# Sample softmax of two heads on 128 partitions, with shared transpositions, in a hybrid encoder step

## The reference, cut to what matters

```python
def fox_block(q, k, v, f_q, f_k, q_pos, k_pos):          # branch B
    s = jnp.einsum('bqhd,bkhd->bhqk', q, k).astype(jnp.float32) * (HEAD_DIM ** -0.5)
    s = s + jnp.swapaxes(f_q, 1, 2)[..., :, None] - jnp.swapaxes(f_k, 1, 2)[..., None, :]
    mask = k_pos[None, :] <= q_pos[:, None]
    s = jnp.where(mask[None, None], s, NEG_INF)
    p = jax.nn.softmax(s, axis=-1).astype(v.dtype)
    return jnp.einsum('bhqk,bkhd->bqhd', p, v)

def band_attention(q, k, v, q_pos, k_pos, rel_bias):     # branch A
    s = jnp.einsum('bqhd,bkhd->bhqk', q, k).astype(jnp.float32) * (HEAD_DIM ** -0.5)
    s = s + rel_bias.astype(jnp.float32)[:, rel][None]
    ...
    p = jax.nn.softmax(s, axis=-1).astype(v.dtype)
    return jnp.einsum('bhqk,bkhd->bqhd', p, v)

# sample: q has 64 rows, k and v have 1024 + 64 (B) or 512 + 64 (A) rows; prompt: 512 rows, causal or banded
```

## Time and profile before

| what | value |
|---|---|
| runs | 2879.72, 2883.22, 2882.98 us |
| profiled execution | 2885.47 us, its span 2883.7 us |
| PE | 2807.5 us busy, 97% of the span |
| PE weight loads | 2641.2 us, 92% |
| DVE | 1320.6 us, 46% |
| ACT | 985.1 us, 34% |
| POOL | 108.6 us, 4% |
| DMA | 112 GB/s mean |

### The profile page before, as it was taken

How to read it: one execution, slowest core, us unless ns; L and a number is a source line. 1 busy time by engine, 2 the same in 40 slices (tenths; PEclk the granted TensorE clock), 3 DMA queues, 4 the chain that set the end, 5 groups by cost and what they waited for, 6 DMA issues and landing times.

```text
span 2883.7 us, 50290 instructions
## 1 busy us (share of the span) xinstructions
PE 2807.5 (97%) x21746; PEld 2641.2 (92%) x21746; DVE 1320.6 (46%) x2597; ACT 985.1 (34%) x1861; POOL 108.6 (4%) x202
## 2 busy tenths in 40 slices
PE   7999999999999999999999999999999999999997
PEld 6999999877899989999999999998778999999997
DVE  3444325666544464443264443256654444644423
ACT  4222224444422352222252222244443224422321
POOL 0000000000000000000000000001000000000000
PEclk9999999999999999999999999999999999999999
DMA  6444532333222234442224445333321222222222
GB/s 242 147 150 155 173 111 86 128 125 104 84 81 81 74 105 151 148 139 85 83 86 153 147 146 169 108 103 124 136 94 59 81 81 81 74 85 84 85 82 69
DMA packets 91084, 324.30 MB, mean 112 GB/s; under 512 B 11232, under 2 KB 14336, under 8 KB 90672
## 3 DMA queue, kind: packets, MB, share of 16 engines
q1 hardware_dynamic: 64048, 222.50, 23.4%
q0 software_dynamic: 26816, 98.59, 10.0%
HBM read 310.16 MB, written 11.55 MB: 112 GB/s over the span
## 4 chain that ended last, share of the span: by engine, by line
PE 84%; DVE 8%; ACT 4%; DVEq 2%; issue 2%; DMA 1%; SPq 0%; POOL 0%; ACTq 0%
PE ps L643 75%; PE ps L757 2%; PE ps L985 2%; PE ps L1018 1%; DVE h L1611 1%; PE ps L998 1%; DVE x_lo L1618 1%; ACT w_hi L1108 1%; ACT prob L1379 1%; DVEq L1610 1%; DVE z L1609 1%; PE ps L652 1%; DMA w_raw<-in_f 1%; ACT sig L1435 1%; DVEq L1926 1%
## 5 line engine op out<-in xcount | busy, mean ns | idle before, releaser
L643 PE MATMUL ps<-x_hi,w_hi 128*128 128x290 f32 (+1 forms) x4256 | 973.3, 304 | 36.1 <-DVE x_lo L1618 13.7
L643 PE MATMUL ps<-x_lo,w_hi 128*128 128x288 f32 (+1 forms) x4256 | 942.4, 297 | 0.0
L643 PE MATMUL ps<-x_hi,w_lo 128*128 128x290 f32 (+1 forms) x4256 | 931.3, 295 | 0.0
L643 PEld LDWEIGHTS ps<-x_hi,w_hi 128*128 128x128 f32 x4256 | 686.9, 189 | 115.3 <-issue 84.5
L643 PEld LDWEIGHTS ps<-x_lo,w_hi 128*128 128x128 f32 x4256 | 697.4, 190 | 0.3
L643 PEld LDWEIGHTS ps<-x_hi,w_lo 128*128 128x128 f32 x4256 | 696.8, 189 | 0.0
L1493 DVE TENSOR_TENSOR w_lo<-w_raw,w_hi 128x1024 fp32r<-128x1024 f32 x386 | 468.8, 1222 | 261.4 <-ACT w_hi L1108 259.1
L1108 ACT CAST w_hi<-w_raw 128x1024 fp32r<-128x1024 f32 x386 | 393.1, 1047 | 82.3 <-DMA w_raw<-in_f 82.3
L643 PE MATMUL ps<-hid_hi,w_hi 128*128 128x288 f32 x1344 | 303.9, 297 | 1.8 <-DVE c_col L1550 1.8
L643 PE MATMUL ps<-hid_hi,w_lo 128*128 128x288 f32 x1344 | 301.6, 295 | 0.0
L643 PE MATMUL ps<-hid_lo,w_hi 128*128 128x288 f32 x1344 | 301.5, 295 | 0.0
(11 more groups left out here) (208 smaller groups left out, 2440.6 us busy)
## 6 DMA issues: line engine op xcount, KB each, us to landing
w_raw<-in_f SPq DMA_DIRECT2D x260, 512.0 KB, 3.5
ada_w<-in_ada POOLq DMA_DIRECT2D x128, 512.0 KB, 5.7
w_raw<-in_gate SPq DMA_DIRECT2D x64, 512.0 KB, 3.5
w_raw<-in_tri SPq DMA_DIRECT2D x42, 512.0 KB, 3.6
decay_s<-f_scratch POOLq DMA_DIRECT2D x8, 1088.0 KB, 7.6
ada_first<-in_ada SPq DMA_DIRECT2D x4, 2048.0 KB, 18.3
w_raw<-in_wout SPq DMA_DIRECT2D x16, 512.0 KB, 3.4
decay_p<-f_scratch POOLq DMA_DIRECT2D x8, 512.0 KB, 5.9
```

Of the source, the lines that this page charges most:

```text
L643: r = mm(ps[:, 2 * out + b, 0:width], w, xx[:, cols(b)], start=first and n == 0, stop=last and n == 2)
```

## The change

The sample's two heads are laid over one another: head 0 on partitions 0 to 63, head 1 on partitions 64 to 127. Unit 2 (`SU`) now stands for both; unit 3 has no softmax of its own.

- PE: the scores of head 1 go to partitions 64 to 127 of the same bank as those of head 0. Segment e uses bank 4 or 5 by its parity, and segments 0 and 1 are issued together, where only segment 0 stood.
- DVE: `sample_logits` works on 128 partitions in B (one instruction a segment where two stood; the diagonal block's decay is prepared in two half instructions), and on two halves in A, since the bias rows of A differ by 64 columns. `normalize` is one of 128 partitions.
- ACT: one exponential of 128 partitions.
- The transpositions are of 128x128, nine in B and five in A, where two times that many of 64x128 stood. They are shared by two turns: `turn(2)` takes blocks 0 to 3, `turn(3)` the rest. `weigh(1)` reads its columns by halves.
- `last_user(5)` is now 3, not 2: slot 2 is free only when both turns are over.
- POOL: `decay_s` is one row on 128 partitions, head 0's on the lower half and head 1's on the upper, by two transfers of half the partitions each.

```diff
-SEGS_A, SEGS_B = 12, 14
+SEGS_A, SEGS_B = 10, 11
...
+SU = 2 * SAMPLE
+S_PART = 4
...
+def sample_blocks(part, cached):
+
+    blocks = [(b, P) for b in range(cached // P)] + [(cached // P, DEC)]
+    return blocks[:S_PART] if part == 0 else blocks[S_PART:]
...
 def last_user(u):
 
-    return u - PROBS if u >= PROBS else max(v for v in range(UNITS) if v % PROBS == u) - UNITS
+    v = u - PROBS if u >= PROBS else max(v for v in range(UNITS) if v % PROBS == u) - UNITS
+
+    return SU + 1 if v == SU else v
...
+    samples_t = prob_t[:, :, :].rearrange("p a n -> p (a n)")
...
-                    mm(score[hh][0:m, 0:c1 - c0], q_st[rows, i * P:i * P + m], k, start=True, stop=True
-                       ).then_inc(scores_ready.sem, 1)
+                    out = score[hh][0:m, 0:c1 - c0] if i < 4 else score[e % 2][rows, 0:c1 - c0]
+                    r = mm(out, q_st[rows, i * P:i * P + m], k, start=True, stop=True)
+                    if i < 4 or hh:
+                        r.then_inc(scores_ready.sem, 1)
...
-                if nb > 8:
-                    pe.wait_ge(o_taken.sem, o_taken.free(l, st * TWINS + u // 2))
+                if u // 2 == SAMPLE:
+                    blocks = sample_blocks(u - SU, cached)
+                    if blocks[-1][0] >= 2 * S_PART:
+                        pe.wait_ge(o_taken.sem, o_taken.free(l, st * TWINS + SAMPLE))
+                    for b, w in blocks:
+                        at = b % S_PART * P
+                        out = turned[0:w, at:at + P] if b < 2 * S_PART else turned_more
+                        r = turn_in(out, prob[:, SU % PROBS, b * P:b * P + w], const[:, IDENT, :])
+                    r.then_inc(prob_turned.sem, 1)
+                    return
...
             scores(SAMPLE)
+            scores(SAMPLE, 1)
             work()
             turn(0)
             work()
-            scores(SAMPLE, 1)
             turn(1)
...
+            def sample_logits(p, own, segs):
+
+                halves = [(hh, slice(hh * HD, hh * HD + HD)) for hh in (0, 1)]
+                if is_b:
+                    dve.wait_ge(decay_s_in.sem, decay_s_in.done(l, st))
+                    for hh, rows in halves:
+                        V.tensor_tensor(own_decay[rows, 0, 0:DEC], decay_s[rows, PAST:SC], mask[rows, CAUSAL, rows],
+                                        ALU.add)
+                    dve.drain()
...
+                    for hh, rows in ((0, slice(0, P)),) if is_b else halves:
...
+                        r = V.tensor_tensor_reduce(prob[rows, p, k0:k1], score[e % 2][rows, 0:k1 - k0], d, -1.0,
                                                    shift if k0 else FAR, ALU.add, ALU.min, shift)
...
                 if u % 2 == 0:
                     normalize(u)
-                    normalize(u + 1)
+                    if u != SU:
+                        normalize(u + 1)
...
                 if u == 1:
-                    expo(2)
-                if 0 < u < UNITS - 2:
+                    expo(SU)
+                if 1 < u < UNITS - 2:
                     expo(u + 2)
```

More of the change, by code:

```diff
@@ L1386, in take_turned @@
                 act.wait_ge(o_summed.sem, o_summed.free(l, st * TWINS + u // 2))
[L1387 to L1392, removed]
+                if i < 4:
+                    r = copy(prob_t[:, hh, 0:nk], turned[:, 0:nk])
+                else:
+                    blocks = sample_blocks(u - SU, cached)
+                    full = [b * P for b, w in blocks if w == P]
+                    if full:
+                        r = copy(samples_t[:, full[0]:full[-1] + P], turned[:, 0:len(full) * P])
+                    b, w = blocks[-1]
+                    if w < P:
+                        src = turned_more if b >= 2 * S_PART else turned[0:w, 0:P]
+                        r = copy(samples_t[0:w, b * P:b * P + P], src)
                 r.then_inc(prob_t_ready.sem, 1)
@@ L1885, in stage, with logits @@
             is_b = cached == PAST
[L1886 removed]
+            def logits(u):
                 hh, i, m, nk, nb, segs = unit_shape(u, cached)
[L1888 to L1894 removed]
+                p = u % PROBS
+                dve.wait_ge(prob_turned.sem, prob_turned.done(l, base + last_user(u)))
@@ L1904, in logits @@
-                for e, (c0, c1) in list(enumerate(segs))[part]:
-                    bank = score[hh]
-                    dve.wait_ge(scores_ready.sem, scores_ready.done(l, seg0 + segment(u, e, cached)))
-                    for k0, k1 in ((c0, nk - m), (nk - m, nk)) if is_b and c0 < nk - m < c1 else ((c0, c1),):
+                if u == SU:
+                    sample_logits(p, nk - m, segs)
+                    return
+                if is_b and u == 0:
+                    dve.wait_ge(decay_p_in.sem, decay_p_in.done(l, st))
@@ new lines, in logits @@
+                if is_b and hh == 0:
+                    causal = mask[:, CAUSAL:CAUSAL + 1, :].to_broadcast((P, 2, P))
+                    V.tensor_tensor(own_decay[:, :, :], decay_p[:, :, i * P:i * P + P], causal, ALU.add)
+                    dve.drain()
+                shift = row[:, SHIFT, p:p + 1]
+                dve.wait_ge(scores_ready.sem, scores_ready.done(l, seg0 + segment(u, 0, cached)))
+                for k0, k1 in ((0, nk - m), (nk - m, nk)) if is_b and nk > m else ((0, nk),):
+                    if not is_b:
+                        d = strip[:, hh, 512 - P * i:512 - P * i + nk]
+                    elif k0 == nk - m:
+                        d = own_decay[:, hh, :]
+                    else:
+                        d = decay_p[:, hh, 0:k1]
+                    if k0:
+                        dve.drain()
+                    r = V.tensor_tensor_reduce(prob[:, p, k0:k1], score[hh][:, k0:k1], d, -1.0,
+                                               shift if k0 else FAR, ALU.add, ALU.min, shift)
```

75 lines of the change are left out of this document (36 added, 39 removed).

## The result

The changed kernel takes 2890.71 us (median of 9 runs, 2887.22 to 2892.27), the kernel before 2882.98 (9 runs, 2879.72 to 2885.02): a ratio of 1.0025, 95% interval 1.0015 to 1.0035. It is slower by a quarter of a percent, though PE's busy time is 9.7 us less. The profiled execution took 2887.69 us.

A forecast was written before the change was run, and what follows sets the result against it. PE was taken as the bound, with a DVE chain ending last behind the sample's second turn. 3.9 us without the clock plus 5.6 for falls made 9.5 over the profiled 2885.47; set on the median, 2892.5 us, range 2880 to 2904.

The forecast's parts named there:

- The slot's wait: DVE: `logits(5)` waits for turn 3, `take_v` and PE behind it; 0.58 us longer per B stage, 0.50 in stage 4.
- the prediction's steps: B stage: turn 2 at 561.57, turn 3 1.36 later, then 0.74, `logits(5)` 0.95, `take_v` to PE's tile 0.97: 565.59.
- one entry and one leaving: PE, sample's first two score segments in one piece: one switch into and out of 64 rows saved, 0.20 us a stage.
- the entry: PE ahead of turn 2 in B: no entry gap for 128 rows, so the turn starts 0.09 us earlier.
- The turns: PE, sample's transpositions in B: four and five replace two times nine, 0.8 us less, 0.1 taken back by waiting.
- the 0.85: Stage 5, where no read of banks follows: PE's own saving stands, 0.85 us with the scores, 1.7 in two layers.
- The sum without the clock: B stages 4.6 us longer, stages 4 1.0 longer, stages 5 1.7 shorter: 3.9 us.
- what waits for DVE between the two segments: PE between the sample's first two score segments: waits no more once they are issued together; counted at nothing.
- The clock: Clock falls behind PE's longer idle waits: five of ten stages, four more than now at 1.4 us, 5.6 us; bounds 0, 12.6.
- The saving: Rival: `take_v` is done when turn 3 is over, so PE keeps its saving; 17 us less, 2866 us; 10 in 100.
- The wait without falls: Rival: the wait grows but the clock holds; 3.9 or 2.5 us more, 2885.5 to 2887 us; 22 in 100.
- Heads apart: Rival: the heads' scores, in halves of one bank, run one behind the other; 20 us more, 2913 us; 8 in 100.

The follow-up runs named there:

- e1: Changed kernel with a slot of its own for the sample's probabilities, three slots of 512 columns rotating over the other eight units: 2869.9 us, ratio 0.9951.
- e2: Changed kernel with `take_v` put ahead of `logits(5)` on DVE in stages 0 to 4, the slot left as it is: 2870.61 us, ratio 0.9954.
- e5: e1 with the sample's second score segment put back between the first two turns: 2874.69 us, ratio 0.9968.
- e6: Kernel before with only the exchange of e2, `take_v` ahead of `logits(5)` on DVE: 2881.15 us, ratio 0.9989.
- e4: Changed kernel with PE's idle time behind the second turn filled by unread transpositions of a constant, 16 in B, 13 in stage 4: 2885.09 us, ratio 1.0004.
- e3: Kernel before with one thing of the change alone, `logits(5)` waiting for turn 3 in place of turn 2: 2911.49 us, ratio 1.0097.
- e10: Changed kernel with nine transpositions of 64 rows of a constant ahead of the sample's second turn, stages 0 to 4: 2903.61 us, ratio 1.0070.
- e11: Changed kernel with eight transpositions of 128 rows of a constant ahead of the sample's second turn, stages 0 to 4: 2898.44 us, ratio 1.0053.
- e9: Changed kernel run again unaltered, for a second profile: 2891.58 us, ratio 1.0023 against the kernel before.
- e7: e1 with the projection tile behind `weigh(0)` moved to behind `weigh(1)` in stages 0 to 4: 2865.19 us, ratio 0.9934.
- e8: Kernel of e3 with the idle time behind turn 3 filled by unread transpositions, 16 in B, 13 in stage 4: 2895.19 us, ratio 1.0039.

## Why the prediction was right, and where its sizes were off

*The slot's wait: right.* `logits(5)` waits for the turns, `take_v` stands behind it, and PE behind `take_v`, in all ten places. e1 and e2 each take away one link and the 20 us go.

*Its size: predicted half as large again as measured.* A B stage got 0.38 us longer (37.43 against 37.05), not 0.58; stage 4 0.27 and 0.22, not 0.50. From the start of the first turn to PE's next tile it took 603.48 - 599.47 = 4.01 us, and the prediction's steps make 565.59 - 561.57 = 4.02. That part was exact in its sum. Off was the start of the chain: the first turn came 0.49 us earlier within stage 1 (598.86 - 583.86 = 15.00 before, 599.47 - 584.96 = 14.51 after), not 0.29. In e5, whose scores stand apart, it comes at 596.45 - 581.61 = 14.84. So the scores gave 0.33 of it, where I had written 0.20 for one entry and one leaving. The other 0.16 came with the new transpositions and the single softmax, where I had written 0.09 for the entry; the 0.07 between I can't place. The term that was mis-sized is in the main that of the scores' piece: I priced the switch from its two edges only, where the whole of two pieces against one could not be read.

*The turns: nearly right.* A saving of 0.7 us in B predicted (0.8 less 0.1), 0.60 measured (e6 against e5). In stage 5 the 0.85 was 0.96: its long wait for c_col came 35.89 us after the stage's start, before 36.85.

*The sum without the clock:* 3.9 us predicted; 8 x 0.38 + 0.27 + 0.22 - 2 x 0.96 = 1.6 measured. By the sums of the ten stages, each profile with one fall, it is 368.85 - 365.67 - 1.92 = 1.3. The 0.3 between lies in stage 3 of layer 1: there PE waited 0.32 us before (at 2099.23, for DVE's row ahead of the sample's third segment of scores), and it doesn't now. The prediction had counted what waits for DVE between the two segments at nothing, and this wait of the third it does not name.

*The clock: right on the size by luck, by a rule that was too simple.* I expected a fall in five stages of ten, four more than before, 5.6 us. Five was a choice between the bounds of 0 and 12.6 us, not a reading. Filled waits give back 5.6 to 6.5 us (e4 against the two medians), while the two profiles show one and four stages, and one of these five falls cost 2.9 us and not 1.4. The rule stood on a wrong reading too. The prediction says that the trace lies just at the edge, a fall behind an idle 0.70 us and none behind 0.68. Stages 2 and 3 of layer 0 of the same trace wait 0.71 us, and both keep the full clock; this is stage 2 of the kernel before, its wait and its window:

```profile
640.51 0.51 PE L643 MATMUL ps<-x_hi,w_hi 128*128 128x288 f32 x2 [0.71 <-DVE c_col L1550]
```
```profile
622.33:659.38 37.05, 35.87 (x294) 28.61 (x293) 23.64 (x82) 17.93 (x47) 3.60 (x6) 1.00 0.38 131
```

So the length of the wait did not decide even there. It doesn't decide alone in the experiments either: the same 1.96 us costs 16 us in e3. The change makes the wait three times as long and at the same time replaces the half-row transpositions that stand ahead of it. By e10 against e11 this hides much of the price; no run takes it alone out of the changed kernel. Nor need the one fall before be typical: the execution profiled there took 2885.47 us, more than any of the nine timed runs.

*The total:* 9.5 us over the kernel before was forecast (2892.5), 7.7 measured (2890.71). The sum without the clock was 2.3 to 2.6 us too large, the clock's part by up to 0.9 too small.

*The rivals.* The saving does not arrive in this form, but it exists: the change without its stall (e1) is 13.9 us faster than before, against the 17 that the rival gave. The wait without falls is what e4 shows, 2885.1: 0.4 us below the 2885.5 to 2887 of that rival, and 1.3 us above its own kernel before, where the rival has 2.5 to 3.9. This fits the sum of 1.3 to 1.6 above. Heads apart: refuted by the starts of the eight matmuls.

The account in medians, along the way from before to after: the exchange on DVE -3.0 (e6), turns and softmax -6.5 (e5 against e6), scores -4.8 (e1 against e5), the slot's wait +15.2 (e4 against e1), the falls +6.5 (e9 against e4), together +7.4; e9 was measured 7.3 above its kernel before. The change saves 11.3 us and the wait, against the old order, costs 12.2; the clock makes the sign plain.

## What to carry to other kernels

When two users of a buffer become one, look at who waits for the buffer now, and then at what stands behind that waiter on its engine: the slot's wait was free in e2 and cost 20 us in the changed kernel, with two steps of one engine exchanged between them. Order an in-order engine so that the reader of the bound engine's banks comes ahead of anything that waits for later work. And where an idle stretch of PE can't be avoided, look at more than one profile: its price in clock differed from execution to execution here, and with what PE did ahead of it.

## What the runs showed of the hardware that I had not expected

- An idle stretch of 1.96 us does not by itself lower the clock: of twenty such or nearly such places (1.62 us in four of them) in two profiles of the changed kernel five were followed by a lower clock. In the kernel before it was one of eight places of 0.68 to 0.71 us.
- The same idle stretch behind transpositions on 64 rows was followed by a lower clock in seven of ten places, twice (e3, e10). One fall of each lasted longer than the others: in stage 2 of e3 the granted clock is 0.50 all the way from 643.1 to 653.2 us, and a stage of 38.3 us became 42.4, at a mean clock of 0.88.
- The fall can come microseconds after the wait. In stage 1 of e3 the granted clock is 1.00 from 604.0 to 605.4 us, right behind the wait, and 0.50 from 605.6 to 608.8. PE's tile ran at full speed, and the scores 2.9 us later slowly (L986, 1.65 us for four matmuls of 64x384 that take 0.92 in e7's last row):

```profile
604.01 0.51 PE L644 MATMUL ps<-x_hi,w_hi 128*128 128x288 f32 x2 [1.96 <-DVE c_col L1551]
...
606.90 1.65 PE L986 MATMUL ps<-k_stage,q_stage 64*128 64x384 f32 x4
```

- Filling the idle time with work that nobody needs made the kernel 5.6 us faster (e4) and 16.3 us faster (e8).
